# Two-block transformer kernel: the weights' splits of the second block's attention rounds moved inside the rounds

## The chip, the cores and the metric

The kernel runs on one core of a Trainium2 chip. The metric is the device time of one execution in microseconds (us), as the median of several runs. PE is TensorE (the matmul engine), DVE is VectorE, ACT is ScalarE, POOL is GpSimd, SP is SyncE, which only issues DMAs here.

## What is computed

The reference applies two transformer blocks to x of shape 512 x 1024 in float32. The change lies in the second block's mixer, so only that is shown:

```python
def _stick_breaking(q, k, v):
    # per head (8 heads of 64) and block of 128 queries
    z = jnp.einsum("bhqd,bhkd->bhqk", qb, kh, preferred_element_type=jnp.float32) * scale
    mask = key_pos[None, :] < q_pos[:, None]
    log_beta = jax.nn.log_sigmoid(z)
    log_1m_beta = jnp.where(mask, jax.nn.log_sigmoid(-z), 0.0)
    between = lax.cumsum(log_1m_beta, axis=3, reverse=True) - log_1m_beta
    attn = jnp.where(mask, jnp.exp(log_beta + between), 0.0)
    return jnp.einsum("bhqk,bhkd->bhqd", attn.astype(vh.dtype), vh)

# second_block: a = rmsnorm(h); u = a @ w_in (1024 x 2560: value, gate, q, k, v)
# mixed = [silu(layernorm(causal conv of 31 taps over value * sigmoid(gate)))), rmsnorm(stick_breaking(q, k, v))]
# h = h + rmsnorm(mixed @ w_out); then a gated MLP of width 2816
```

## The kernel before, in words

**Products.** Every float32 product is made of three matmuls of rounded parts (`mm3`, lines 1060 to 1062): high by high, high by low, low by high. So each weight has to be split on the chip before PE can use it. A slab is one load of 128 x 1024 weights. SP loads it into one of four raw buffers; ACT rounds it into WH (`weights` in the scalar program, line 1763); DVE writes the rest, raw minus WH, into WL (`weights` in the vector program, line 2237). There are three WH/WL pairs, used in turn, so slab i can be rounded only when slab i-3 has been used. PE takes the slabs in their order (`next_slab`, line 1055) and waits there until DVE has written the whole slab's low part. A slab of the second block's input weights, and one of its output weights, is split in two halves: two instructions of 128x512 on ACT and two on DVE.

**Order.** No engine chooses at run time. The list PLAN_C (lines 620 to 679) names the steps of the second block's mixer in one order; the PE, ACT and DVE programs each walk that list and do what a step means for them. An instruction that waits for a semaphore holds up all behind it on its engine. A step `("w", n)` means nothing to PE; on ACT and DVE it splits all slabs below number n that aren't split yet.

**Rounds.** After the 13 first tiles of the input projection and the value rows (`v2`, four slabs) come eight rounds, one for each head u. The order within round u before the change, with the engine and line of each step, is:

- `ev` (DVE, line 2753): if the round before made a tile of the projection (k2, q3 or k3) in PSUM bank 7, evict it; for u = 4 to 6 `co` (line 2813) evicts a part of the convolution instead
- `lg u` (PE lines 1547 and 1060 to 1062; ACT lines 2099, 2101, 2103): logits, then ACT's Abs (three), Exp and Ln for the softplus. ACT waits before the Abs until DVE has read the buffer LN_ of the round before (line 2805)
- `taps` (DVE, line 2730, and 2727 for a channel's first): steps of the convolution on DVE, two here
- in later rounds `ps`, `pt` (PE lines 1617, 1622; DVE 2824) for the norm of a pair of heads, and `dg` (DVE, line 2770), the diagonal matrices for the part of the convolution that PE does
- `bt u-1` (PE, line 1564): cumulative sums of the softplus of the round before, 20 matmuls for its high part and 20 for its low part
- `va u-2` (PE): the product with the values
- `sp u` (DVE, line 2801, three): the softplus' sum
- `ex u-1` (ACT, line 2114, three): the exponent
- `lo` (ACT line 2088, DVE line 2790): high and low part of the tile evicted in this round
- in rounds 4 and 6 `pr` and `px`: the reciprocal root for a pair
- `taps` (two), then `sl u`: ACT rounds the softplus (line 2108), DVE writes its low part (line 2805)
- `ah`, `at` of u-1: the same for the attention weights (ACT 2120, DVE 2809), and `kp u-2` (ACT 2126)
- `BEHIND[u]` (PE): the tile k2, q3 or k3 of the projection in rounds 0, 1 and 2 (24 matmuls; each waits in `next_slab` for its slab and in `free_7` for the eviction of what bank 7 held before), then a third of the convolution in rounds 3, 4 and 5 (`conv_group`, which waits for the diagonals), nothing after that
- `w`: in round 0 the slabs of q3 and k3, in rounds 1, 2 and 3 one slab of the output weights each
- `pl` and the last `taps` of the round (one in rounds 0 to 2, else three)

The slab of k2 is split earlier, in the steps of the value rows. The first of the output weights' slabs is used behind the last round.

Of the kernel before, what the change touches and what calls it, by code (L numbers as in the profile page):

```python
# [97 lines left out]
def build(nc, cols, ins, out):  # L98
# [71 lines left out]
    SL, CH = {}, {}  # L170
# [449 lines left out]
    PLAN_C = []  # L620
# [12 lines left out]
    for u in range(8):  # L633
        b = BEHIND[u - 1] if u else ("", "")
        if b[0] == "tile":
            PLAN_C += [("ev", b[1])]
        elif b[0] == "cv":
            PLAN_C += [("co", b[1])]
        PLAN_C += [("lg", u), ("taps", 2)]
        if u >= 4:  # L640
            PLAN_C += [("pt" if u % 2 else "ps", u // 2 - 2)]
        if BEHIND[u][0] == "cv":
            PLAN_C += [("dg", u - 3)]
        if u == 6:
            PLAN_C += [("ln_add",)]
        if u == 7:
            PLAN_C += [("ln_q", j) for j in range(4)]
        if u >= 1:
            PLAN_C += [("bt", u - 1)]
        if u == 6:  # L650
            PLAN_C += [("ln_sub",)]
        if u >= 2:
            PLAN_C += [("va", u - 2)]
        PLAN_C += [("sp", u)]
        if u >= 1:
            PLAN_C += [("ex", u - 1)]
        if b[0] == "tile":
            PLAN_C += [("lo", b[1])]
        if u >= 4 and u % 2 == 0:
            PLAN_C += [("pr", u // 2 - 2), ("px", u // 2 - 2)]  # L660
        if u == 6:
            PLAN_C += [("ln_dv",)]
        if u == 7:
            PLAN_C += [("ln_qa", 1), ("ln_qa", 2)]
        PLAN_C += [("taps", 2), ("sl", u)]
        if u >= 1:
            PLAN_C += [("ah", u - 1), ("at", u - 1)]
        if u >= 2:
            PLAN_C += [("kp", u - 2)]
        PLAN_C += [BEHIND[u]]  # L670
        if u < 5:
            PLAN_C += [("w", CH["v2"].last + min(u, 3) + 4)]
        if u >= 4 and u % 2:
            PLAN_C += [("pl", u // 2 - 2)]
        PLAN_C += [("taps", 1 if u < 3 else 3)]
# [2339 lines left out]
```

## Time and profile before

| | |
|---|---|
| median of 3 runs | 1763.02 us (1762.97 to 1763.67) |
| the profiled execution | 1763.04 us |
| its span | 1761.2 us, mean granted TensorE clock 0.993 |
| PE busy | 1719.3 us (98%) |
| DVE busy | 1256.6 us (71%) |
| ACT busy | 818.4 us (46%) |
| the eight rounds | from about 1237 to 1345 us of the span |

Times in the views are us from the span's start. A row of the timeline gives start, duration of the merged instructions, engine, line, operation, output and input, count, and in square brackets how long the engine was idle before and what ended that. The durations of merged rows run from the first start to the last end, so consecutive instructions overlap by their pipelining.

### The profile page before, as it was taken

The page shows a single profiled execution, that of the slowest core. Times are in us where ns is not written, and L with a number is a line of the kernel's source. Part 1 is how long each engine was busy: PE and PEld are TensorE (multiplying, and loading weights), DVE is VectorE, ACT ScalarE, POOL GpSimd, SP SyncE. Part 2 cuts the span into 40 slices and gives each one's busy share as a digit, 9 for nine tenths or more (in the row PEclk, how much of TensorE's full clock was granted, in tenths as well). Part 3 has the DMA queues.
Part 4 walks back from the last instruction along what each step waited for, and adds up shares of the span by engine and source line. Part 5 has one row for each costly group of instructions (what it writes and reads, how often), then busy time and mean ns, then how long its engine had stood idle before and what let it go on. Part 6 is the DMA issues. An engine that isn't in the chain of part 4 may idle for free.

```text
span 1761.2 us, 21518 instructions
## 1 busy us (share of the span) xinstructions
PE 1719.3 (98%) x8215; PEld 1416.3 (80%) x8215; DVE 1256.6 (71%) x1915; ACT 818.4 (46%) x1345; POOL 38.0 (2%) x87
## 2 busy tenths in 40 slices
PE   8999999999999999999999999999999999999998
PEld 7887888888888777778888888778888788888886
DVE  6666358687887667775778788889987644765766
ACT  7433244343445656664444343542767532333342
POOL 0000000000001121000000000000000000000000
PEclk9999999999999999999999999999999999999999
DMA  7222442333412112115152423033100353224212
GB/s 250 84 72 84 129 134 80 114 97 106 141 39 65 61 51 71 37 49 180 51 147 66 143 72 120 12 96 101 55 13 7 91 178 96 72 87 143 69 49 84
DMA packets 195749, 158.29 MB, mean 90 GB/s; under 512 B 5248, under 2 KB 161280, under 8 KB 195648
## 3 DMA queue, kind: packets, MB, share of 16 engines
q1 hardware_dynamic: 194240, 154.16, 28.8%
q0 software_dynamic: 400, 1.25, 0.3%
q8 instruction: 65, 1.06, 0.3%
q10 hardware_dynamic: 1008, 1.53, 0.2%
q14 instruction: 36, 0.29, 0.1%
HBM read 154.81 MB, written 2.10 MB: 89 GB/s over the span
## 4 chain that ended last, share of the span: by engine, by line
PE 89%; DVE 6%; ACT 3%; issue 1%; DMA 0%; POOL 0%; DVEq 0%; SPq 0%; ACTq 0%
PE ps L1060 28%; PE ps L1062 28%; PE ps L1061 28%; PE ps L1564 1%; PE ps L1130 1%; ACT sb L2020 1%; DVE sb L2237 1%; ACT sb L1763 1%; PE ps L1453 0%; DVE sb L2494 0%; DVE sb L2235 0%; DVE sb L2263 0%; PE ps L1189 0%; DVE sb L2730 0%; ACT sb L1769 0%
## 5 line engine op out<-in xcount | busy, mean ns | idle before, releaser
L1060 PE MATMUL ps<-sb,sb 128*128 128x512 f32 (+3 forms) x2435 | 928.7, 388 | 9.7 <-ACT sb L2020 5.2
L1062 PE MATMUL ps<-sb,sb 128*128 128x512 f32 (+3 forms) x2435 | 912.6, 380 | 0.0
L1061 PE MATMUL ps<-sb,sb 128*128 128x512 f32 (+3 forms) x2435 | 912.2, 379 | 0.0
L2237 DVE TENSOR_TENSOR sb<-sb,sb 128x1024 fp32r<-128x1024 f32 (+1 forms) x414 | 404.8, 997 | 219.2 <-ACT sb L1763 218.4
L1060 PEld LDWEIGHTS ps<-sb,sb 128*128 128x128 f32 (+1 forms) x2435 | 451.5, 188 | 110.1 <-issue 11.7
L1763 ACT ACTIVATE sb<-sb 128x1024 fp32r<-128x1024 f32 (+1 forms) x414 | 349.7, 871 | 394.5 <-PE ps L1062 389.2
L1062 PEld LDWEIGHTS ps<-sb,sb 128*128 128x128 f32 (+1 forms) x2435 | 451.1, 188 | 86.8
L1061 PEld LDWEIGHTS ps<-sb,sb 128*128 128x128 f32 (+1 forms) x2435 | 451.6, 188 | 82.4 <-issue 0.2
L2477 DVE TENSOR_TENSOR sb<-sb,sb 128x1024 fp32r<-128x1024 f32 x70 | 85.5, 1221 | 47.5 <-ACT sb L1925 45.2
L1920 ACT ACTIVATE sb<-sb 128x512 f32<-128x512 f32 x64 | 40.3, 630 | 130.8 <-DVE sb L2529 130.8
L2459 DVE TENSOR_TENSOR sb<-sb,sb 128x1024 f32<-128x1024 f32 x80 | 95.1, 1216 | 0.6
L2494 DVE TENSOR_TENSOR sb<-ps,sb 128x512 f32<-128x512 f32 x120 | 76.1, 681 | 0.0
L2730 DVE SCALAR_TENSOR_TENSOR sb<-sb,sb,sb 128x512 f32<-128x512 f32 x90 | 67.4, 749 | 1.9
L1925 ACT ACTIVATE sb<-sb 128x1024 fp32r<-128x1024 f32 x56 | 58.7, 1048 | 9.2 <-DVE sb L2471 9.1
L2529 DVE SCALAR_TENSOR_TENSOR sb<-ps,sb 128x512 f32<-128x512 f32 x64 | 43.6, 684 | 9.0 <-PE ps L1062 9.0
L2471 DVE TENSOR_TENSOR sb<-sb 128x1024 f32<-128x1024 f32 x40 | 48.7, 1216 | 0.1
L2193 ACT ACTIVATE sb<-sb 128x512 f32<-128x512 f32 x22 | 13.9, 632 | 72.6 <-DVE sb L2936 72.5
L2263 DVE SCALAR_TENSOR_TENSOR sb<-ps,sb,sb 128x512 fp32r<-128x512 f32 (+1 forms) x48 | 31.0, 700 | 13.6 <-ACT sb L1782 13.6
L2235 DVE SCALAR_TENSOR_TENSOR sb<-sb,sb,sb 128x512 fp32r<-128x512 f32 x40 | 29.5, 747 | 8.8 <-ACT sb L1763 8.5
L1130 PE MATMUL ps<-sb,sb 128*128 128x128 f32 x176 | 27.2, 295 | 8.7 <-DMA sb<-in_con 5.0
L1130 PEld LDWEIGHTS ps<-sb,sb 128*128 128x128 f32 x176 | 22.1, 150 | 14.4 <-DMA sb<-in_con 5.0
L1769 ACT ACTIVATE sb<-sb 128x1024 f32<-128x1024 f32 x26 | 27.6, 1061 | 10.3 <-DVE sb L2684 4.8
(217 smaller groups left out, 1109.3 us busy)
## 6 DMA issues: line engine op xcount, KB each, us to landing
sb<-in_w_up SPq DMA_DIRECT2D x86, 512.0 KB, 4.1
sb<-in_w_down SPq DMA_DIRECT2D x86, 512.0 KB, 4.9
sb<-in_w_gate SPq DMA_DIRECT2D x22, 512.0 KB, 3.9
sb<-in_a_w_in SPq DMA_DIRECT2D x20, 512.0 KB, 3.8
sb<-in_w_in SPq DMA_DIRECT2D x20, 512.0 KB, 3.7
sb<-in_w_o SPq DMA_DIRECT2D x16, 512.0 KB, 3.7
sb<-in_w_mem_kv SPq DMA_DIRECT2D x8, 512.0 KB, 7.6
sb<-in_w_out SPq DMA_DIRECT2D x8, 512.0 KB, 3.8
```

The source lines that it names most:

```text
L1060: mm(ps, lh, rh, start=start, stop=False, **k)
L1061: mm(ps, lh, rl, start=False, stop=False, **k)
L1062: return mm(ps, ll, rh, start=False, stop=stop, **k)
L1130: i = e.transpose(banks[4 + k % 4][:, 128 * t:128 * t + 128], src[:, t, 128 * k:128 * k + 128], IDENT)
L1763: act(WH[i % N_SPLIT][:, a], raw[:, a], ACT.Copy, scale=g).then_inc(S("w_hi"), parts)
L1925: act(AR[(7 * g + j) % 4][0], a_of(l, g, j)[0], ACT.Copy).then_inc(S("h_hi"), 1)
L2237: tt(lo, raw, hi, ALU.subtract).then_inc(S("w_lo"), parts)
L2459: tt(db[d][a][:, :], db[b][a][:, :], db[c][a][:, :], ALU.subtract).then_inc(S("t_sum"), 1)
L2471: tt(d, x, y, op).then_inc(S("hs"), 1)
L2477: tt(lo, a_of(l, g, j)[0], hi.bitcast(F32), ALU.subtract).then_inc(S("h_lo"), 1)
L2494: tt(x, y, x, ALU.add).then_inc(S("res"), 1)
L2730: stt(CV[:, j, :], GL[:, j, k:k + T], col("convw", 4 * k + j), CV[:, j, :], ALU.mult, ALU.add).then_inc(S("tap"), 1)
```

## The change

The step `w` leaves the end of the rounds 0 to 4 and is put into the rounds 1 to 5, behind `sp u` (DVE) and `ex u-1` (ACT), ahead of `lo`, `pr` and `sl u`. Round 1 now splits the slabs of q3 and k3, the rounds 2, 3 and 4 split a slab of the output weights each, and round 5's step finds nothing left to split, as round 4's did before.

```diff
         PLAN_C += [("sp", u)]
         if u >= 1:
             PLAN_C += [("ex", u - 1)]
+        if 1 <= u < 6:
+
+            PLAN_C += [("w", CH["v2"].last + min(u - 1, 3) + 4)]
         if b[0] == "tile":
             PLAN_C += [("lo", b[1])]
...
         PLAN_C += [BEHIND[u]]
-        if u < 5:
-            PLAN_C += [("w", CH["v2"].last + min(u, 3) + 4)]
         if u >= 4 and u % 2:
             PLAN_C += [("pl", u // 2 - 2)]
         PLAN_C += [("taps", 1 if u < 3 else 3)]
```

`CH["v2"].last` is the last of the value rows' slabs; it is followed by the slabs of k2, q3, k3 and then those of the output weights.

## Rows read from the trace of the kernel before

**Rows 1.** The page: busy time, share of the span, instructions, by engine.

```profile
PE 1719.3 (98%) x8215; PEld 1416.3 (80%) x8215; DVE 1256.6 (71%) x1915; ACT 818.4 (46%) x1345; POOL 38.0 (2%) x87
```

**Rows 2.** Waits before PE, whole span: total, times, longest (us).

```profile
PE ps L1564 <- ACT sb L2108: 3.6, 1, 3.6
...
PE ps L1060 <- DVE sb L2753: 1.8, 1, 1.8
```

**Rows 3.** PE's timeline: end of the sums of round 1, start of tile q3.

```profile
1248.77 2.45 PE L1564 MATMUL ps<-sb,sb 128*128 128x256 f32 x16
1253.04 0.50 PE L1060 MATMUL ps<-sb,sb 128*128 128x512 f32 x1 [1.81 <-DVE sb L2753]
```

**Rows 4.** DVE's timeline, end of round 0 to round 2.

```profile
1247.68 1.63 DVE L2805 TENSOR_TENSOR sb<-sb,sb 128x1408 fp32r<-128x1408 f32 x1
1249.23 2.49 DVE L2237 TENSOR_TENSOR sb<-sb,sb 128x512 fp32r<-128x512 f32 x4
...
1252.30 0.68 DVE L2753 SCALAR_TENSOR_TENSOR sb<-ps,sb 128x512 f32<-128x512 f32 x1
...
1254.35 1.75 DVE L2801 SCALAR_TENSOR_TENSOR sb<-ps,sb 128x512 f32<-128x512 f32 x3
...
1258.06 1.62 DVE L2805 TENSOR_TENSOR sb<-sb,sb 128x1408 fp32r<-128x1408 f32 x1
1259.59 1.62 DVE L2809 TENSOR_TENSOR sb<-sb,sb 128x1408 fp32r<-128x1408 f32 x1
...
1265.05 1.75 DVE L2801 SCALAR_TENSOR_TENSOR sb<-ps,sb 128x512 f32<-128x512 f32 x3
```

**Rows 5.** ACT's timeline, end of round 0 and round 1.

```profile
1247.56 2.18 ACT L1763 ACTIVATE sb<-sb 128x512 fp32r<-128x512 f32 x4
1249.64 1.44 ACT L2099 ACTIVATE sb<-ps 128x512 f32<-128x512 f32 x3
...
1252.52 1.38 ACT L2103 ACTIVATE sb<-sb 128x1408 f32<-128x1408 f32 x1
1253.81 1.45 ACT L2114 ACTIVATE sb<-ps 128x512 f32<-128x512 f32 x3
...
1256.13 1.39 ACT L2108 ACTIVATE sb<-sb 128x1408 fp32r<-128x1408 f32 x1 [0.35 <-DVE sb L2801]
```

**Rows 6.** The chain of waits, by time: start, us, what.

```profile
1261.20 3.02 PE ps L1564 x20
...
1289.39 4.47 PE ps L1564 x20
...
1310.53 0.24 PE ps L1060
...
1321.59 2.94 PE ps L1564 x20
1324.61 1.47 ACT sb L2114 x3
...
1338.67 5.49 PE ps L1564 x20
```

**Rows 7.** Stretches: width, busy us of the engines, granted clock, DMA.

```profile
1289.90:1293.30 3.40, 3.40 (x15) 3.26 (x15) 3.40 (x6) 1.93 (x2) 0.00 (x0) 0.52 0.01 4
...
1337.60:1341.00 3.40, 2.33 (x9) 2.24 (x10) 3.25 (x4) 3.35 (x4) 0.00 (x0) 0.50 0.00 0
1341.00:1344.40 3.40, 3.40 (x17) 3.30 (x15) 2.01 (x3) 0.83 (x3) 0.00 (x0) 0.51 0.00 0
```

**Rows 8.** ACT's timeline, round 4.

```profile
1293.95 1.47 ACT L2114 ACTIVATE sb<-ps 128x512 f32<-128x512 f32 x3 [2.09 <-PE ps L1564]
...
1296.92 1.37 ACT L2108 ACTIVATE sb<-sb 128x1408 fp32r<-128x1408 f32 x1
```

**Rows 9.** DVE's timeline, rounds 4 to 6.

```profile
1306.49 3.15 DVE L2770 TENSOR_TENSOR sb<-sb,sb 128x1408 fp32r<-128x1408 f32 x2
...
1318.22 0.69 DVE L2813 TENSOR_TENSOR sb<-ps,sb 128x512 f32<-128x512 f32 x1 [1.05 <-PE ps L1062]
```

## The prediction, on record before the changed kernel ran

> **What bounds the kernel now.** The busy times come first: PE works for 98% of the span, DVE 71%, ACT 46% [rows 1]. So the question for any change of order is only where PE idles, and what it would newly wait for. The table of waits before PE has, for the rounds, two entries: 3.6 us ahead of the last head's sums, waiting for ACT's rounded softplus, and 1.8 us ahead of one tile, waiting for the eviction by L2753 [rows 2]. PE's timeline puts the second at the end of round 1: the sums end at 1251.22, the tile of q3 starts at 1253.04 [rows 3]. DVE's timeline says why. Bank 7 still holds k2, and the eviction of k2 stands in DVE's list behind the low part of round 0's softplus (until 1249.31) and the four halves of the splits of q3 and k3 (2.49 us); it runs from 1252.30 to 1252.98, and PE starts 0.06 us later [rows 3, 4]. Elsewhere in the rounds until 1335 PE does not wait. The end of the second wait, 1338.67, follows from PE's own sums of round 6 (end 1324.53), from which the chain goes to ACT's exponent at 1324.61 and on [rows 6]: a delay of PE before that is not absorbed there, it moves the whole chain.
>
> **What is moved.** Five slabs, ten halves on ACT and ten on DVE, none added or removed. Round 1 now splits q3 and k3 behind `sp 1` and `ex 0`; rounds 2, 3, 4 split an output slab each. The decisive point is in the lists: PE's `BEHIND[1]` is the tile of q3, and it waits for both low halves of q3's slab. Before, they were written a round earlier; now they stand on DVE behind a softplus that can't start before ACT's Abs, Exp and Ln of head 1.
>
> **Round 1, step by step.**
> - Gain: DVE goes from the low part (1249.31) by one tap (0.7 us) to the eviction of k2, done at about 1250.7, ahead of PE's 1251.22. The wait of 1.8 us on the eviction goes. The one that is late next is the split.
> - ACT has no splits behind round 0's rounding. Its Abs waits for DVE's read of the same buffer, done at 1249.31, so it starts at about 1249.35 where it started at 1249.64 [rows 4, 5]: 0.3 us earlier. Ln, which ended at 1252.52 + 1.38 = 1253.90, ends at 1253.6 [rows 5].
> - ACT then does the three exponents of head 0 (1.45 us; the sums they need end at 1251.22): until 1255.0. The rounding of q3's two halves follows; four took 2.18 us, so two take 1.1, less 0.1 of overlap: done at 1256.0 [rows 5].
> - DVE does `sp 1` from 1253.65 to 1255.4 (1.75 us), waits for ACT, and does two halves at 2.49/4 = 0.62 us each; the second can begin at about 1256.05 and its 0.68 us end at 1256.75 [rows 4].
> - PE starts the tile of q3 about 0.06 us later, 1256.8 to 1256.9, where it was 1253.04: **+3.8 us**. Bounds: if ACT's rounding never held DVE up, 1255.4 + 1.25 = 1256.65 gives +3.7; if all four halves had to pass ACT first, 1255.0 + 2.2 + 0.7 = 1257.9 gives +4.9. I take 3.8, the lists name each waiter.
>
> **PE's clock.** PE is then idle for 5.6 us in one piece, from 1251.2 to 1256.85. The nearest row is the wait of 3.6 us before 1338.67: from 1337.6 the granted clock was half (0.50 and 0.51 in two stretches, 6.8 us together, that is 1.2 instead of 2.4 GHz), and the 20 matmuls of the sums took 5.49 us, where in round 2 they took 3.02 [rows 6, 7]: 2.5 us lost. Bounds: nothing, since 1.8 us of idle in this very place left the clock full; and half of 6.8 us = 3.4 us, if PE works through all of such a stretch. The idle time here is longer than the 3.6 us, so I take **+2.4 us**.
>
> The Trainium skill, "TensorE: Matmul & The Clock Gate", section "Terms", prices a slow stretch at its whole duration times one minus the clock's ratio. By that the two stretches would cost 3.4 us and the total would be 1 us higher than mine. The trace does not agree for its own case: the measured 2.5 us are less, because PE idled through the first third of the slow time (2.33 of 3.40 us busy) [rows 7].
>
> **Rounds 2 and 3.** These exchange one slab at their end for one in their middle. DVE's total between two softpluses is the same. The rounding of the softplus moves back by 1.1 us on ACT; in round 1 it moves from 1256.13 to 1257.6, its low part from 1258.06 to about 1260, the weights' low part from 1259.59 to 1261.5. PE needs the high part at 1261.20 at the earliest, and that moves by the 3.8 us and more [rows 4, 5, 6]: hidden by over 5 us. If that cover were gone, it would cost 1.1 us a round. Cost nothing.
>
> **Rounds 4 and 5.** Round 4 had no split ahead of its rounding and gets one, and the pair's root stands behind it. From ACT's exponents (end 1295.42 [rows 8]) two halves add 1.1 us there and the following DVE work, two halves of 0.62 us, comes out 1.2 to 1.5 us later. The next thing on DVE that PE needs soon is the second set of diagonals in round 5, 1306.49 to 1309.64; PE begins the last third of the convolution at 1310.53, 0.9 us later [rows 6, 9]. So 0.3 to 0.6 us of it reach PE: **+0.5 us** (bounds: 0 and 1.5). The rest ends in DVE's idle 1.05 us before 1318.22 [rows 9].
>
> **DMAs and other queues.** The loads of two output slabs wait on SP for the low parts of q3 and k3 and start some 6 us later; their own splits come a round and more behind, and nothing else in these rounds waits for a load. POOL has no step here. Cost nothing; the cover is a round of about 13 us (between the softpluses at 1254.35 and 1265.05 alone are 10.7 us [rows 4]).
>
> **Sum.** 3.8 + 2.4 + 0.5 = 6.7 us, against the profiled execution's own 1763.04 us: 1769.7 us. The median of the runs (1763.02) is the same within 0.02 us. I say 1769.6.
>
> **The rivals.** About 0.2% (3.5 us) is what a measurement of this kernel can tell from no change.
> - *As forecast*, split and slow clock: 1767.5 to 1771.5. Chance 0.62.
> - *The clock does not fall, or the delay moves a later slow stretch off the work.* Before, head 3's sums took 4.47 us instead of 3.02, at a clock of 0.52 without any idle time of PE's ahead [rows 6, 7]; such a stretch may fall elsewhere once all is moved. 3.8 + 0.5 = 4.3 us gives 1767.3; with 1.45 us back from head 3's sums, 2.9 us, 1765.9, which is no measurable change. Against it: 5.6 us of idle in one piece. Chance 0.17, half of it within 0.2%. The Trainium skill (the same page, section "What's actually happening") says that the place of the slow time is not tied to the kernel and varies from run to run; by it this rival weighs more than my one row would give it. The runs here, within 0.7 us of each other, don't show a large variation.
> - *More is lost*: all 1.5 us of round 4's DVE delay reach PE, and the slow clock lasts through the tile and the logits (3.4 us): 3.8 + 3.4 + 1.5 = 8.7 us, 1771.8, and 1773.4 with a further slow stretch of 1.6 us. For it: DVE's merged rows from 1247.68 to 1265.05 carry no idle time in brackets [rows 4]. Chance 0.13.
> - *Faster*: the place is round 1's tile of q3. If the low halves of q3 land before PE ends the sums (1251.22), the eviction's 1.8 us are all gained, the stages behind get the 0.3 us of the earlier Abs, and with the slow stretch off head 3's sums another 1.45: 3.55 us, 1759.5. It decides at 1251.22; for that the splits would have to precede Ln's end at 1253.6, against the lists' order. Chance 0.03.
> - *The change does nothing*, because another wait covers it (1.8 us won, as much lost): 1763.0. Chance 0.05.
>
> **How the numbers follow.** Likeliest 1769.6. The range leaves out the fast cases and the far end: 1765.8 (3.8 + 0.5 - 1.45 = 2.9, rounded) to 1772.4. Chances: slower 0.62 + 0.13 + 0.09 = 0.84; within 0.2% 0.08 + 0.05 = 0.13; faster 0.03.
>
> **What the profile after would show.** In the waits before PE, the 1.8 us on L2753 replaced by one of about 5.6 us on DVE L2237, before L1060, from about 1251.2 to 1256.9. In DVE's timeline the eviction of k2 at about 1250, then an idle piece of some 1.6 us before L2801 at 1253.65, and four halves behind it. A clock of 0.5 on the tile of q3 or the logits of head 2, so that from the start of that tile to the next head's sums it is over 10 us instead of 8.2 (1253.04 to 1261.20). From there all of the rounds later by about 6 us, the 3.6 us wait before the last sums unchanged, the diagonals of round 5 ending just as PE needs them. The forecast is wrong if PE's wait before q3 is below 4 us, if the clock stays full, or if the wait at 1335 shrinks by what was lost before.

## The result and the profile after

| | before | after |
|---|---|---|
| median of 6 runs each | 1762.99 us (1760.77 to 1763.67) | 1768.60 us (1768.03 to 1769.63) |
| profiled execution | 1763.04 us | 1768.65 us |
| its span | 1761.2 us | 1766.8 us |

By the medians the changed kernel takes 5.6 us more. The ratio on record is 1.0042 (95% interval 1.0032 to 1.0051), that is 7.4 us more (5.6 to 9.0). It is not the quotient of these two medians, which is 1.0032, the lower end of its interval; how it is formed is not on record. Below, ratios are compared only with ratios. The forecast was 6.6 us more, between the two.

The page after, its span and busy times. All code lines behind the added ones have a number higher by one: L1060 is L1061, L2237 is L2238, and so on.

```profile
span 1766.8 us, 21518 instructions
...
PE 1719.9 (97%) x8215; PEld 1416.5 (80%) x8215; DVE 1257.2 (71%) x1915; ACT 818.6 (46%) x1345; POOL 38.0 (2%) x87
```

PE's busy time has grown by 0.6 us only, DVE's and ACT's by 0.6 and 0.2 [rows 1]: the work is the same. PE's busy time does not show the slow clock that the change brings (2.4 us, below), because slow stretches elsewhere, which the execution before had, are missing here. The waits before PE, whole span (total, times, longest):

```profile
PE ps L1061 <- DVE sb L2238: 6.2, 2, 5.8
...
PE ps L1565 <- ACT sb L2109: 3.6, 1, 3.6
...
PE ps L1623 <- DVE sb L2814: 1.1, 1, 1.1
```

The wait of 1.8 us on the eviction [rows 2] is gone. In its place stands one of 5.8 us on the split's low part; the 3.6 us before the last head's sums are unchanged; one of 1.1 us on line 2814, the eviction of a third of the convolution, is new. DVE's timeline from the end of round 0 to round 2, to be laid beside [rows 4]:

```profile
1247.99 1.63 DVE L2806 TENSOR_TENSOR sb<-sb,sb 128x1408 fp32r<-128x1408 f32 x1
1249.54 0.75 DVE L2731 SCALAR_TENSOR_TENSOR sb<-sb,sb,sb 128x512 f32<-128x512 f32 x1
1250.20 0.68 DVE L2754 SCALAR_TENSOR_TENSOR sb<-ps,sb 128x512 f32<-128x512 f32 x1
1250.80 1.53 DVE L2731 SCALAR_TENSOR_TENSOR sb<-sb,sb,sb 128x512 f32<-128x512 f32 x2
1253.97 1.75 DVE L2802 SCALAR_TENSOR_TENSOR sb<-ps,sb 128x512 f32<-128x512 f32 x3 [1.64 <-ACT sb L2104]
1255.85 2.50 DVE L2238 TENSOR_TENSOR sb<-sb,sb 128x512 fp32r<-128x512 f32 x4
...
1260.31 1.61 DVE L2806 TENSOR_TENSOR sb<-sb,sb 128x1408 fp32r<-128x1408 f32 x1
```

The eviction of k2 (L2754) is over at 1250.88, before PE's sums end at 1251.53. Then DVE idles for 1.64 us until ACT's Ln is done, makes the softplus' sum, and only then the four low halves. ACT's timeline beside [rows 5], and PE's first matmul of the tile of q3:

```profile
1249.65 1.47 ACT L2100 ACTIVATE sb<-ps 128x512 f32<-128x512 f32 x3 [1.69 <-DVE sb L2806]
...
1252.56 1.38 ACT L2104 ACTIVATE sb<-sb 128x1408 f32<-128x1408 f32 x1
1253.85 1.45 ACT L2115 ACTIVATE sb<-ps 128x512 f32<-128x512 f32 x3
1255.17 2.19 ACT L1764 ACTIVATE sb<-sb 128x512 fp32r<-128x512 f32 x4
...
1257.77 1.38 ACT L2109 ACTIVATE sb<-sb 128x1408 fp32r<-128x1408 f32 x1
```

```profile
1257.28 0.77 PE L1061 MATMUL ps<-sb,sb 128*128 128x512 f32 x1 [5.75 <-DVE sb L2238]
```

ACT's Abs starts behind DVE's read at 1249.62, Ln ends at 1253.94, the exponents at 1255.30; the first two of the four rounded halves are done by about 1256.3 and PE starts at 1257.28. The clock behind that wait, in stretches of the whole core (width, busy us of PE, PEld, DVE, ACT, POOL, granted clock, DMA):

```profile
1252.50:1255.90 3.40, 0.00 (x0) 0.00 (x0) 1.81 (x4) 3.37 (x7) 0.00 (x0) 0.97 0.00 0
1255.90:1259.30 3.40, 2.02 (x5) 1.66 (x6) 3.40 (x6) 3.40 (x6) 0.00 (x0) 0.50 0.21 58
1259.30:1262.70 3.40, 3.40 (x10) 2.63 (x9) 3.36 (x4) 1.12 (x1) 0.00 (x0) 0.52 0.70 250
1262.70:1266.10 3.40, 3.40 (x19) 2.50 (x18) 2.01 (x3) 0.00 (x0) 0.00 (x0) 1.00 0.00 0
1296.00:1299.40 3.40, 3.40 (x24) 3.22 (x24) 3.36 (x7) 2.81 (x3) 0.00 (x0) 1.00 0.00 0
```

PE does nothing from 1252.5 to 1255.9, and then the granted clock is half, 1.2 GHz, for 6.8 us. The first twelve matmuls of the tile fall into it; they start 0.43 us apart, the ones behind them 0.23 us. From the first matmul of the tile to head 1's sums PE needs 1267.84 - 1257.28 = 10.56 us, where it was 1261.20 - 1253.04 = 8.16 [rows 3, 6]: 2.40 us lost. The last row is head 3's sums: this time at the full clock (before, 0.52 [rows 7]). Rounds 4 and 5 on DVE, on ACT and in the chain of waits:

```profile
1301.60 1.28 DVE L2238 TENSOR_TENSOR sb<-sb,sb 128x512 fp32r<-128x512 f32 x2
...
1310.64 0.69 DVE L2814 TENSOR_TENSOR sb<-ps,sb 128x512 f32<-128x512 f32 x1
...
1313.35 3.15 DVE L2771 TENSOR_TENSOR sb<-sb,sb 128x1408 fp32r<-128x1408 f32 x2
```

```profile
1299.10 1.47 ACT L2115 ACTIVATE sb<-ps 128x512 f32<-128x512 f32 x3 [0.55 <-PE ps L1565]
1300.44 1.16 ACT L1764 ACTIVATE sb<-sb 128x512 fp32r<-128x512 f32 x2
...
1303.40 0.63 ACT L2140 ACTIVATE sb<-sb 128x512 f32<-128x512 f32 x1 [1.46 <-DVE sb L2254]
1303.93 1.36 ACT L2109 ACTIVATE sb<-sb 128x1408 fp32r<-128x1408 f32 x1
```

```profile
1255.85 1.30 DVE sb L2238 x2
...
1310.64 0.70 DVE sb L2814
...
1311.38 0.66 PE ps L1623 x4
1312.04 2.83 PE ps L1565 x20
...
1345.03 4.37 PE ps L1565 x20
```

ACT's exponents now have the splits behind them, and the rounding of the softplus comes 4.83 us behind the exponents' start, where it was 2.97 [rows 8]. Both halves of the split lie in this way: 1.16 us on ACT, and 1.28 us on DVE ahead of the pair's root, for which ACT's `px` (L2140) waits 1.46 us (0.64 us before). DVE reaches the eviction L2814 only at 1310.64, and PE waits for bank 7 until 1311.38.

Along PE's rows the difference to before adds up as follows: 0.3 us when the sums of head 0 end (1251.22 to 1251.53), 6.6 at head 1's sums (3.94 from the longer wait, 2.40 from the clock), 6.3 at the first pair's transposes in round 5 (1305.12 to 1311.38; 1.1 more by the new wait, 1.5 less by head 3's sums at full clock), 6.4 at the start of the last sums, 5.2 at their end (they took 4.37 us instead of 5.49), 5.6 at the end of the span. So the 5.6 us of this pair of executions are 7.7 us of loss up to round 5 (0.3 of them from ahead of the change's first step), less 2.6 us that slow stretches took in the execution before and not in this one, and about half a microsecond behind the rounds.

### The profile page after: what moved, and what is told of

It reads as the page before. It is cut to its first block, busy times and chain, and to the rows that moved or that the text cites. A ratio compares the mean times of both kernels' runs of the same rounds, so it can differ in the third digit from the quotient of the medians.

```text
span 1766.8 us, 21518 instructions
## 1 busy us (share of the span) xinstructions
PE 1719.9 (97%) x8215; PEld 1416.5 (80%) x8215; DVE 1257.2 (71%) x1915; ACT 818.6 (46%) x1345; POOL 38.0 (2%) x87
## 4 chain that ended last, share of the span: by engine, by line
PE 87%; DVE 7%; ACT 4%; issue 1%; DMA 0%; POOL 0%; DVEq 0%; SPq 0%; ACTq 0%
PE ps L1061 28%; PE ps L1063 27%; PE ps L1062 27%; DVE sb L2731 1%; PE ps L1131 1%; DVE sb L2238 1%; ACT sb L2021 1%; PE ps L1565 1%; ACT sb L1764 1%; PE ps L1454 0%; DVE sb L2495 0%; DVE sb L2236 0%; DVE sb L2802 0%; PE ps L1078 0%; PE ps L1190 0%
## 5 line engine op out<-in xcount | busy, mean ns | idle before, releaser
L1061 PE MATMUL ps<-sb,sb 128*128 128x512 f32 (+3 forms) x2435 | 929.8, 388 | 13.6 <-DVE sb L2238 6.2
L2238 DVE TENSOR_TENSOR sb<-sb,sb 128x1024 fp32r<-128x1024 f32 (+1 forms) x414 | 404.9, 998 | 219.3 <-ACT sb L1764 218.2
L1061 PEld LDWEIGHTS ps<-sb,sb 128*128 128x128 f32 (+1 forms) x2435 | 452.2, 189 | 114.0 <-issue 17.8
L1783 ACT ACTIVATE sb<-ps,sb 128x512 fp32r<-128x512 f32 (+1 forms) x48 | 28.1, 658 | 10.4 <-PE ps L1131 10.4
```

Source lines behind the costliest of these rows:

```text
L1061: mm(ps, lh, rh, start=start, stop=False, **k)
L2238: tt(lo, raw, hi, ALU.subtract).then_inc(S("w_lo"), parts)
```

## The experiments

Theory A: PE waits for q3's own split (and the clock falls behind that wait); the other moves cost only through DVE's lag in round 5. Rival B: splits ahead of the softplus' rounding are dear in every round. Rival C: the slow clock has nothing to do with the wait. Rival D: the wait of round 5 is a lag from round 1. Rival E: DVE sets the pace, and what PE wins at one place it loses at the next. Ratios are to the kernel before on the same chip, whose median there was 1761.1 to 1761.3 us; differences between kernels are therefore taken between ratios, 0.001 being 1.76 us. Each trace is one execution. "Changed" is the changed kernel; it was not run again beside the experiments. The edits are shown against the changed kernel, unless another is named. The steps' helper lines move by one to seven.

### q3k3_alone: only q3 and k3 move

```diff
-        if 1 <= u < 6:
+        if u == 1:
...
-            PLAN_C += [("w", CH["v2"].last + min(u - 1, 3) + 4)]
+            PLAN_C += [("w", CH["v2"].last + 4)]
...
         PLAN_C += [BEHIND[u]]
+        if 1 <= u < 4:
+            PLAN_C += [("w", CH["v2"].last + u + 4)]
```

> Only the splits of q3 and k3 move into round 1; the output slabs stay at the ends of rounds 1 to 3. Theory A (PE's tile of q3 waits for its own split, and the clock falls behind that wait; the other moves cost about 1 us through DVE in round 5): the wait before the tile of q3 stays about 5.7 us, the 1.1 us wait of round 5 on the convolution's eviction is gone, 1767.5 us (1766.5 to 1768.6). Rival B (the splits ahead of the softplus' rounding are what costs, in every round): most of the loss is gone, 1764.5 us or less.

Ratio 1.0029 (1.0018 to 1.0039). Waits before PE in the rounds (1235 to 1345 us), the one of interest:

```profile
PE ps L1063 <- DVE sb L2240: 5.8, 1, 5.8
```

The wait on the split is the same, that of round 5 is gone, and the tile of q3 with the logits takes 10.48 us (1256.52 to 1267.00), so the clock fell here too (0.50 and 0.51 in two stretches of 3.4 us from 1254.90). By the ratio it is 5.1 us above before; theory A had 4.5 (3.5 to 5.6), B 1.5 or less. B, as what makes most of the loss, is out. It is also 2.3 us below the changed kernel by the ratios, of which the wait of round 5 explains 1.1; the intervals of the two ratios overlap.

### outs_alone: only the output slabs move

```diff
-        if 1 <= u < 6:
+        if 2 <= u < 5:
...
-            PLAN_C += [("w", CH["v2"].last + min(u - 1, 3) + 4)]
+            PLAN_C += [("w", CH["v2"].last + u + 3)]
...
         PLAN_C += [BEHIND[u]]
+        if u == 0:
+            PLAN_C += [("w", CH["v2"].last + 4)]
```

> The splits of q3 and k3 go back to the end of round 0; the three output slabs stay inside rounds 2 to 4. Theory A: the wait of 1.8 us on the eviction of k2 is back, none on a split, a wait of about 1.1 us in round 5, 1764.1 us (1763.0 to 1765.2). Rival B: still slow, 1767 us or more.

Ratio 0.9997 (0.9988 to 1.0005).

```profile
PE ps L1063 <- DVE sb L2756: 1.8, 1, 1.8
PE ps L1625 <- DVE sb L2816: 1.1, 1, 1.1
```

Both waits are where and as long as expected. The time is not: 0.5 us below before instead of 1.1 above, with an interval that reaches 0.9 us above it. The 1.1 us can't be seen in the time here; that this part costs nothing like 5 us can. This kernel has no lag from round 1, and it has the wait of round 5; q3k3_alone had the lag and not the wait. So the wait comes from the output slabs inside the rounds, and rival D is out.

### after_pe_filled: the wait filled with work of no use

```diff
                 n = IN_FIRST.index(a[0]) if a[0] in IN_FIRST else -1
+                if a[0] == "q3":
+                    for r in range(22):
+                        mm(banks[7][:, :], Ah[:, 0, 0:128], Ah[:, 0, :], start=True, stop=True)
```

> The changed kernel with 22 matmuls of 128x512 of no use put on PE ahead of the tile of q3, behind the eviction of k2; they fill about 5 us of the 5.75 us wait. Theory A with the clock's fall caused by the idle time: the tile of q3 starts at the same time as in the changed kernel, but at the full clock, so that from its start to head 1's sums it is 8.2 us instead of 10.6: 1766.2 us (1765.5 to 1767.7, the upper end if a slow stretch of 1.4 us comes back later). Rival C (the slow stretch has nothing to do with the wait): 1768.6 us as in the changed kernel, or more.

Ratio 1.0020 (1.0011 to 1.0028), beside 1.0042 (1.0032 to 1.0051) for the changed kernel, which was timed on another occasion. PE's timeline at the place, and two stretches (columns as above):

```profile
1249.63 5.17 PE L1599 MATMUL ps<-sb 128*128 128x512 f32 x22
1255.46 0.50 PE L1061 MATMUL ps<-sb,sb 128*128 128x512 f32 x1 [0.66 <-DVE sb L2241]
```

```profile
1254.40:1257.80 3.40, 2.74 (x12) 1.94 (x11) 3.40 (x6) 3.40 (x6) 0.00 (x0) 1.00 0.29 78
1257.80:1261.20 3.40, 3.40 (x19) 2.63 (x18) 3.37 (x4) 0.90 (x1) 0.00 (x0) 1.00 0.65 230
```

The 22 matmuls take the place of 5.2 us of the wait, 0.66 us of it is left, and the clock stays at 1.00. From the tile's start to head 1's sums it is 1263.58 - 1255.46 = 8.12 us. All three traced kernels with the wait of 5.75 us (changed, q3k3_alone, last_out_in_round3) have half clock for 6.8 us on the tile behind it, and this one has none. So the slow clock of the changed kernel came from the idle time, and its price at this place is 10.56 - 8.12 = 2.4 us. Rival C is out.

The tile did not start at the same time as in the changed kernel, as expected, but 1.8 us earlier (1255.46 and 1257.28). The whole stage was entered earlier: head 0's sums began at 1246.71 instead of 1248.45. The trace of the changed kernel has two stretches of 3.4 us at half clock from 702.4 and 712.6, the one here has the full clock there (last section). In the whole time the ratios differ by 0.0022, 3.9 us; those 1.7 us and the 2.4 us together are about that much, and only the 2.4 us belong to the wait.

### q3_stays: q3's split goes back

```diff
         PLAN_C += [BEHIND[u]]
+        if u == 0:
+            PLAN_C += [("w", CH["v2"].last + 3)]
```

> Only q3's split goes back to the end of round 0, k3's is made in round 1 and the output slabs in rounds 2 to 4. Theory A: the eviction of k2 stands behind two halves instead of four, the wait before q3's tile is 0.6 us (1.8 - 1.25), the wait of round 5 about 1.1 us: 1762.9 us (1761.5 to 1764.5). Rival B: 1767 us.

Ratio 1.0000 (0.9991 to 1.0008).

```profile
PE ps L1063 <- DVE sb L2773: 0.9, 1, 0.9
PE ps L1063 <- DVE sb L2756: 0.6, 1, 0.6
PE ps L1625 <- DVE sb L2816: 0.6, 1, 0.6
```

One slab at the end of round 0 instead of none takes the whole loss away. The wait before the tile of q3 is 0.6 us, as worked out; that of round 5 is 0.6 us and not the expected 1.1 (see the table below). But 0.9 us of a new wait has come on L2773, the first diagonals: PE is earlier by what it won, DVE is not. The sum of the three waits is 2.1 us against 1.8 before.

### last_out_in_round3 and split_behind_eviction

Against the changed kernel, first `last_out_in_round3`, then `split_behind_eviction`:

```diff
-        if 1 <= u < 6:
+        if 1 <= u < 4:
...
-            PLAN_C += [("w", CH["v2"].last + min(u - 1, 3) + 4)]
+            PLAN_C += [("w", CH["v2"].last + u + 3)]
...
         PLAN_C += [BEHIND[u]]
+        if u == 3:
+            PLAN_C += [("w", CH["v2"].last + 7)]
```

```diff
             PLAN_C += [("ev", b[1])]
+        if u == 1:
+            PLAN_C += [("w", CH["v2"].last + 4)]
...
-        if 1 <= u < 6:
+        if 2 <= u < 6:
```

> The changed kernel, with the last of the three output slabs split at the end of round 3 (as before the change) instead of inside round 4. Theory A: the wait of 5.75 us before the tile of q3 and the slow clock behind it stay, the wait of 1.1 us in round 5 on the convolution's eviction goes: 1.1 us faster than the changed kernel, ratio to before about 1.0035 (0.6 thousandths less than the changed kernel's). Rival D (the 1.1 us is no effect of the split inside round 4 but of DVE's lag since round 1): the wait of round 5 stays.

Ratio 1.0043 (1.0030 to 1.0055). Waits before PE in the rounds:

```profile
PE ps L1063 <- DVE sb L2240: 5.8, 1, 5.8
PE ps L1567 <- ACT sb L2111: 3.6, 1, 3.6
```

PE's timeline at head 3's sums:

```profile
1294.79 4.60 PE L1567 MATMUL ps<-sb,sb 128*128 128x256 f32 x20
```

The wait of round 5 is gone, as theory A has it. Head 3's sums were slow here, though, which holds up PE more than DVE, so this trace alone would not prove it. The other traces do, by the time from the end of head 3's sums to the end of the eviction that round 5's transposes wait for; PE is ready for them 11.3 us after the sums in each:

| kernel | split inside round 4 | head 3's sums, us | eviction done after them, us | PE's wait, us |
|---|---|---|---|---|
| changed | yes | 3.07 | 12.3 | 1.1 |
| outs_alone | yes | 3.07 | 12.3 | 1.1 |
| q3_stays | yes | 4.59 | 11.9 | 0.6 |
| q3k3_alone | no | 3.07 | 11.1 | 0 |
| last_out_in_round3 | no | 4.60 | 10.8 | 0 |
| before | no | 4.61 | 10.5 | 0 |

At the same speed of the sums the split inside round 4 makes the eviction 1.1 or 1.2 us later. The time has not fallen by 1.1 us, though. In this execution head 3's sums took 4.60 us and the last head's 5.49 us from 1344.18, where the changed kernel had 3.07 and 4.37: in this execution slow stretches took back the 1.1 us and more. The mechanism is shown, its worth in the time is not.

> The splits of q3 and k3 stand in round 1 directly behind the eviction of k2, ahead of the logits' step, so DVE no longer has to wait for ACT's Ln before them; the output slabs stay as changed. Theory A: PE waits for q3's low halves until about 1252 us, 0.7 us instead of 5.75, the clock does not fall: ratio to before 0.999 to 1.001. Rival B (any split within a round is dear): 1.003 or more.

Ratio 1.0001 (0.9992 to 1.0010).

```profile
PE ps L1625 <- DVE sb L2816: 1.2, 1, 1.2
PE ps L1063 <- DVE sb L2240: 0.7, 1, 0.7
```

The same splits in the same round, ahead of the wait for Ln instead of behind it: 0.7 us of wait instead of 5.8, as worked out, and 7.2 us less by the ratios. What costs is the place behind Ln, not the round.

### best_guess and best_dg_first: without the wait for q3

`best_guess` against `last_out_in_round3`, then `best_dg_first` against `best_guess`:

```diff
             PLAN_C += [("ev", b[1])]
+        if u == 1:
+            PLAN_C += [("taps", 1)]
...
         PLAN_C += [BEHIND[u]]
+        if u == 0:
+            PLAN_C += [("w", CH["v2"].last + 3)]
...
-        PLAN_C += [("taps", 1 if u < 3 else 3)]
+        PLAN_C += [("taps", 0 if u == 0 else 1 if u < 3 else 3)]
```

```diff
-        PLAN_C += [("lg", u), ("taps", 2)]
+        PLAN_C += [("lg", u)] + [("dg", 0)] * (u == 3) + [("taps", 2)]
...
-        if BEHIND[u][0] == "cv":
+        if u in (4, 5):
             PLAN_C += [("dg", u - 3)]
```

> q3's split at the end of round 0, the tap behind it moved behind the eviction of k2, k3's split inside round 1, the output slabs inside rounds 2 and 3 and the last at the end of round 3. Theory A: no wait before q3's tile (at most 0.1 us), the wait of round 5 gone, but PE then comes 0.6 us earlier to the first diagonals than in the kernel that keeps q3's split, where it waited 0.94 us for them: 1.5 us there. Ratio to before 0.9995 to 1.0. With rival B 1.002 or more.

Ratio 1.0004 (0.9996 to 1.0013).

```profile
PE ps L1067 <- DVE sb L2777: 1.6, 1, 1.6
```

No wait before q3's tile, and 1.6 us at the diagonals: the waits are as expected. The ratio is a little above the expected 0.9995 to 1.0, with an interval that covers it.

> The kernel before this one, with the first diagonals ahead of round 3's two taps on DVE (1.5 us). Theory A: the wait for the diagonals goes too, all of the 1.8 us of before's wait are won: ratio to before 0.999 (0.9985 to 0.9998). Rival E (DVE sets the pace of the rounds, what is won at one place is lost at the next): 1.0.

Ratio 0.9999 (0.9990 to 1.0008).

```profile
PE ps L1629 <- DVE sb L2820: 1.4, 1, 1.4
PE ps L1067 <- DVE sb L2250: 1.0, 1, 1.0
PE ps L1067 <- DVE sb L2777: 0.2, 1, 0.2
```

My theory A missed here. The diagonals come in time, but 1.0 us is waited for the root of the first pair (L2250, round 4) and 1.4 us for the convolution's eviction (L2820, round 5): 2.6 us together. Rival E fits: PE comes earlier, DVE's list up to round 5 is as long as before. The next run tests it.

### taps_later: less work on DVE before round 5

Against `best_dg_first`:

```diff
-        PLAN_C += [("taps", 0 if u == 0 else 1 if u < 3 else 3)]
+        PLAN_C += [("taps", (0, 1, 1, 1, 1, 3, 3, 3)[u])]
```

> The kernel with the first diagonals ahead, and four steps of DVE's convolution taken from the ends of rounds 3 and 4 (two each, 3 us of DVE) to the end of round 5 and round 6, where DVE idled. Rival E, now the theory (DVE's work up to round 5 sets the pace once PE's wait for q3 is gone): the waits of 0.99 us on the pair's root in round 4 and of 1.43 us on the convolution's eviction in round 5 go, so that 0.2 to 0.5 us of waits are left in rounds 1 to 5, against 1.8 us before: ratio to before 0.9990 (0.998 to 0.9997). Its rival (these waits come from ACT or from PE's own order): they stay, 2.4 us, ratio 1.0.

Ratio 0.9983 (0.9974 to 0.9992), median 1758.31 us beside 1761.31 us of before.

```profile
PE ps L1571 <- ACT sb L2115: 3.6, 1, 3.6
```

All waits of PE's in rounds 1 to 5 are gone; the 3.6 us before the last sums are the only one left between 1235 and 1345 us. So DVE's work did set the pace, as rival E has it. DVE's four steps had room behind round 4, where it had idled in rounds 5 and 6 [rows 9]. This version is ahead of both kernels: 1.8 us by the waits, about 3 us by the ratio, the interval from 1.4 to 4.6 us (that of best_dg_first, taken on another chip, overlaps it slightly). The time gained beyond the waits may come from the clock: in this trace it is half for 3.4 us between 1235 and 1345 us, in that of before for 10 us. One trace each does not show that this is the kernel's doing.

## Why the prediction was right, step by step

- **The wait before the tile of q3** (predicted 5.6 us in place of 1.8, +3.8): 5.75 us in place of 1.81, +3.94. The eviction of k2, Ln, the exponents, the rounding and the low halves came in the predicted order; the 0.1 us more lies in small gaps (the second low half ends at 1257.15, and PE starts 0.13 us later, not 0.06). outs_alone, q3k3_alone and split_behind_eviction show that this one place makes the loss, all but what round 5 adds.
- **The clock** (predicted +2.4 us, with bounds of 0 and 3.4): +2.40 us at the place, and after_pe_filled shows that the idle time caused it. The page's price in the Trainium skill ("TensorE: Matmul & The Clock Gate", section "Terms", duration times one minus the ratio) would be 3.4 us for the 6.8 us; as in the last sums of before, the trace has less. PE was idle for 1.38 us of the slow time, and a slow matmul starts 0.43 us after the one before it, not twice the 0.23 us of a fast one; twelve times 0.20 us is 2.4. (The prediction says that PE idled through the first third of the slow time before the change; by its row it was 1.07 of 6.8 us. Its sum does not use this.)
- **Rounds 2 and 3 cost nothing**: right. In the changed kernel PE waits nowhere between 1257.28 and 1310.
- **Round 5** (predicted +0.5 us at the diagonals): mis-sized and misplaced. The step that failed is "The next thing on DVE that PE needs soon is the second set of diagonals in round 5". An earlier thing was needed sooner: the eviction L2814, which round 5's transposes wait for because they use the same bank 7; it came 1.1 us late, and the diagonals were then just in time. The 1.1 us are within the stated bounds of 0 and 1.5, and the split's own share, 1.2 us between q3k3_alone and outs_alone, is what the prediction had for DVE. What it had not is that PE's slack at this eviction was there only while head 3's sums were slow: with them at the full clock it is 0.1 us (q3k3_alone), before it was 0.8 us.
- **What the sum lacked**: slow stretches elsewhere. The sum 3.8 + 2.4 + 0.5 = 6.7 had nothing for head 3's sums (1.5 us won, as the second rival had it), the last sums (1.1 us won) and what lies behind the last sums (about 0.4 us lost, with 6.8 us at half clock in the next stage from 1406.0 where it was 3.4 us from 1402.5). With the measured 3.94 + 2.40 + 1.10 and the 0.3 us by which the stage was entered later that makes 5.5; the span has 5.6. That the medians came out 1 us under the sum of 6.7 and not over it is luck: the terms that belong to the change measured 7.4 us, and which stretches are slow differs between executions. The ratio on record, 7.4 us, agrees with the three terms.
- **DMAs**: no wait on one in the rounds, right.
- **The slow rival** (8.7 us) failed in its clock term, 2.4 and not 3.4; **the fast rival** failed at its own condition, the low halves landed 5.6 us behind the end of the sums.

## What to carry to other kernels

Before a step is moved within a fixed order, look up the first consumer on every engine, not only the one that the move is meant to relieve: here a wait of 1.8 us went and one of 5.75 came, since the split was put behind the softplus' long chain on ACT while its consumer stayed where it was. A long wait of PE's costs more than its length, here 2.4 us on 3.9. And where one engine has no idle time, removing a single wait of the other moved it here to the next meeting point (1.8 us became 1.6, then 2.6); only work taken away from the full engine, four steps into its idle time, removed the waits.

## What the runs showed of the hardware that was not expected

- The slow clock also comes without any idle time of PE's ahead of it: head 3's sums in the kernel before and in last_out_in_round3, at 4.6 us instead of 3.07, both times right behind the pair's sums (line 1617), eight matmuls of only 2 columns. q3_stays and best_guess have the same at the same place (clock 0.57 over 3.4 us). In the changed kernel the same matmuls stand there and the clock stayed full, so they are not enough for it; what is, is open.
- Behind the wait of 1.8 us the clock stayed full before. In outs_alone, with the same wait at the same place (until 1249.76), it was full for about 1.2 us more and then half, which cost 1.6 us up to the next sums. Whether the wait brought it is open, since a slow stretch also comes without one:

```profile
1251.00:1254.40 3.40, 3.40 (x9) 2.63 (x8) 3.37 (x7) 3.06 (x6) 0.00 (x0) 0.51 0.34 117
```

- Executions of one kernel differ by more than the first three suggested: before ranged from 1757.1 to 1765.2 us over 31 runs, where the first three had lain within 0.7 us. Slow stretches that come and go are the likely cause. The Trainium skill says of the same clock ("TensorE: Matmul & The Clock Gate", section "What's actually happening") that where the slow time falls is not tied to the kernel's start; the two traces that follow agree. They show one such pair of stretches where the kernels are the same: until late in round 1 outs_alone has the steps of before, and its head 0's sums begin 3.3 us earlier (1244.87 and 1248.14). From 702.4 and 712.6 the trace of before is at half clock for 3.4 us each, with PE busy throughout; first before, then outs_alone:

```profile
702.40:705.80 3.40, 3.40 (x15) 2.90 (x14) 0.99 (x2) 1.03 (x2) 0.11 (x1) 0.53 0.35 132
712.60:716.00 3.40, 3.40 (x13) 2.77 (x12) 1.93 (x8) 3.07 (x8) 0.00 (x0) 0.54 0.26 99
```

```profile
702.40:705.80 3.40, 3.23 (x32) 2.89 (x30) 1.33 (x4) 0.69 (x1) 0.00 (x0) 1.00 0.14 53
712.60:716.00 3.40, 3.40 (x22) 2.52 (x21) 3.10 (x7) 2.60 (x8) 1.29 (x1) 1.00 0.00 0
```

The changed kernel's trace is slow at both places too, that of after_pe_filled at neither. So two single executions can differ by some 3 us before any change is made.

- So a mechanism of about 1 us shows clearly in the waits and not in the time, even with five rounds: removing the 1.1 us wait gave 1.0043 beside 1.0042.
